# Gate and up projections of a feed-forward layer as seven block products instead of eight

## The chip, the cores and the metric

The kernel runs on one core of one Trainium2 chip. The core has TensorE (PE in the rows, its weight loads PEld), VectorE (DVE), ScalarE (ACT), GpSimd (POOL) and the DMA queue of SyncE (SP). Every engine works through its own list of instructions in order, and the engines meet at semaphores. The metric is the time of one execution on the device in microseconds (us), the median of several runs.

## The reference, cut to what matters

One layer of a hybrid decoder over 528 tokens (16 learned ones in front of 512), width 1024, hidden width 2816:

```python
h = h + mixed @ w_o                       # w_o: 1024 x 1024
gt, up = jnp.split(rms_norm(h, norm2) @ w_gate_up, 2, axis=-1)   # each 512 x 2816
return h + (jax.nn.silu(gt) * up) @ w_down                        # w_down: 2816 x 1024
...
return rms_norm(h, final_norm)[:, N_META:]
```

`mixed` comes from a gated delta rule with eight heads and a short convolution. That part takes some 60% of the time and the change leaves it alone. `rms_norm` multiplies by a factor for each token (the inverse root of the mean square) and by a weight for each channel. The kernel applies the token's factor behind the product: rows of `gt` and `up` are scaled by it, after `h` times the channel weight has gone through TensorE.

## The kernel before, in words

Everything lies transposed: channels on the 128 partitions, tokens along the free axis. A weight block is 1024 inputs by 128 outputs, stored as 128 x 1024: eight tiles (k = 0 to 7) of 128 x 128. The list BLOCKS orders all blocks: projections of the mixers, then eight `wo` blocks (the product with w_o), then 22 pairs of a `gate` and an `up` block. After these MAIN blocks comes the product with w_down, in 22 more blocks of the stream, for eight tiles of output channels (m = 0 to 7) with 22 inner tiles each (k = 0 to 21, one for each pair).

For precision every operand is used as a sum of two fp32r values, a high part and a low part. A product of one weight tile with 512 tokens is then three matmuls of 512 columns (`products`): high weights by high tokens, high by low, low by high. A block is 8 x 3 = 24 matmuls, a pair 48.

A weight block goes through four engines. SP loads it into `w_raw` (three buffers), ACT rounds each half (128 x 512) to `w_hi`, POOL subtracts for `w_lo` (`split_weights` on both, L416 and L330 of the rows), and TensorE waits for the low part of the half. `w_hi` and `w_lo` have two buffers each, so the halves of block n+1 are made while TensorE computes block n.

The loops on ACT, DVE and POOL go through the same n: in each step q = 0 to 3 an engine does a piece of the delta rule, a piece of the evacuation of block n-1 (`evacuate`), and (q = 1, 2) a half of the weights of block n+1. So on ACT the work on the result of block n-1 stands ahead of the weights of block n+1.

The evacuations that matter here: for `wo` block m, DVE adds the result to `h1` (L987), ACT writes the scaled `og_hi` (L626), DVE the low part `og_lo` (L989), ACT the squares `sqt` (L630), which POOL adds up in `sqa`. TensorE sums them over the channels with a matmul of ones (`h_sums`) inside the first `up` block, and ACT makes the token factor `rs2` of it (L418, L419). For `gate`, DVE multiplies by `rs2` (`tg`), ACT takes silu (`sg`, L635), DVE multiplies by `rs2` once more. For `up`, DVE multiplies the result by `sg` (`ff`), ACT rounds to `f_hi` and POOL subtracts for `f_lo` (L380). In the product with w_down, DVE adds each finished tile to `h1` (L1027); the last tile is done in two halves of 256 tokens, so that the final norm of the first half can start early.

## Time and profile before

| | |
|---|---|
| median of 3 runs | 1071.83 us (1071.82 to 1072.09) |
| the profiled execution | 1071.95 us |
| its span (first to last instruction) | 1070.1 us |
| TensorE busy | 1058.5 us, 99% of the span |
| VectorE, ScalarE, GpSimd busy | 417.6, 426.9, 538.3 us |
| TensorE's granted clock over the span | 0.997 of full speed |

The span and what lies around it (1.85 us) make the profiled time. In the rows, a start is counted from the start of the span. The time of a matmul in a row runs from its start to its modelled end, and matmuls overlap; the distance from one start to the next tells what one costs. The same holds, to a smaller degree, for instructions that follow each other on DVE, ACT and POOL.

### The profile page before, as it was taken

Reading aid. Unit: us, or ns where it says so; the run is one execution under the profiler, and the core shown is the slowest. Engines: PE = TensorE matmul, PEld = TensorE weight load, DVE = VectorE, ACT = ScalarE, POOL = GpSimd, SP = SyncE. Lnnn points to the kernel's source line nnn. Section 1 sums busy time; section 2 is a strip of 40 time slices with the busy share of each in tenths; the row PEclk is TensorE's granted clock in tenths of the full one; section 3 lists DMA queues with packets and bytes.
Section 4 is the critical chain, followed back from the end, with each engine's and each line's share of the span. In section 5 each row is a group of like instructions: output and inputs, shape, how many; then the busy total and the mean of one; then the engine's idle time right before and its main releaser. Section 6 shows DMA issues by size and latency. Waiting matters only on the chain.

```text
span 1070.1 us, 20296 instructions
## 1 busy us (share of the span) xinstructions
PE 1058.5 (99%) x8233; PEld 902.9 (84%) x8233; DVE 417.6 (39%) x771; ACT 426.9 (40%) x957; POOL 538.3 (50%) x467
## 2 busy tenths in 40 slices
PE   8999999999999999999999999999999999999996
PEld 8989898989999999978888888878888888888886
DVE  6575757576676767643211122221111211100002
ACT  7736354545545354534222334433223332233222
POOL 0163636363635454453645546755555555555553
PEclk9999999999999999999999999999999999999998
DMA  6221222121222121222522333223222332232222
GB/s 224 71 90 63 70 78 72 60 90 61 76 75 71 61 90 61 73 68 79 177 99 79 99 98 96 84 97 99 99 84 94 99 99 93 86 98 98 99 79 79
DMA packets 28812, 95.44 MB, mean 89 GB/s; under 512 B 2984, under 2 KB 5288, under 8 KB 28720
## 3 DMA queue, kind: packets, MB, share of 16 engines
q1 hardware_dynamic: 27520, 91.77, 26.4%
q10 hardware_dynamic: 1200, 2.38, 0.6%
q8 instruction: 65, 1.06, 0.4%
q14 instruction: 27, 0.22, 0.1%
HBM read 92.03 MB, written 2.11 MB: 88 GB/s over the span
## 4 chain that ended last, share of the span: by engine, by line
PE 97%; ACT 1%; DVE 1%; issue 0%; DMA 0%; DVEq 0%; SPq 0%; ACTq 0%
PE bank L1045 96%; DMA h_in<-h_t 0%; PE bank L1245 0%; PE bank L1239 0%; DVE w_lo L719 0%; ACT w_hi L416 0%; DVE cv L878 0%; DVE raw L708 0%; ACT x_hi L425 0%; ACT L484 0%; ACT L651 0%; DVE h L1036 0%; PE bank L1252 0%; PE bank L1251 0%; ACT qkv L651 0%
## 5 line engine op out<-in xcount | busy, mean ns | idle before, releaser
L330 POOL TENSOR_TENSOR w_lo<-w_raw,w_hi 128x512 fp32r<-128x512 f32 x312 | 410.2, 1332 | 480.7 <-ACT w_hi L416 480.6
L1045 PE MATMUL bank<-x_hi,w_hi 128*128 128x258 f32 (+2 forms) x896 | 247.7, 334 | 0.4 <-DVE w_lo L719 0.4
L1045 PE MATMUL bank<-x_hi,w_lo 128*128 128x258 f32 (+2 forms) x896 | 230.1, 315 | 0.0
L1045 PE MATMUL bank<-x_lo,w_hi 128*128 128x258 f32 (+2 forms) x896 | 228.0, 315 | 0.0
L416 ACT ACTIVATE w_hi<-w_raw 128x512 fp32r<-128x512 f32 x322 | 187.6, 618 | 91.8 <-PE bank L1045 91.6
L1045 PE MATMUL bank<-og_hi,w_hi 128*128 128x512 f32 x416 | 164.7, 396 | 0.0
L1045 PE MATMUL bank<-og_lo,w_hi 128*128 128x512 f32 x416 | 164.3, 395 | 0.0
L1045 PE MATMUL bank<-og_hi,w_lo 128*128 128x512 f32 x416 | 164.3, 395 | 0.0
L1045 PEld LDWEIGHTS bank<-x_hi,w_lo 128*128 128x128 f32 x896 | 147.3, 189 | 11.3
L1045 PEld LDWEIGHTS bank<-x_hi,w_hi 128*128 128x128 f32 x896 | 146.0, 189 | 12.4 <-DVE w_lo L719 0.7
L1045 PEld LDWEIGHTS bank<-x_lo,w_hi 128*128 128x128 f32 x896 | 146.3, 189 | 8.9
L1045 PEld LDWEIGHTS bank<-og_lo,w_hi 128*128 128x128 f32 x416 | 78.0, 187 | 19.3 <-issue 0.2
L1045 PEld LDWEIGHTS bank<-og_hi,w_hi 128*128 128x128 f32 x416 | 78.0, 187 | 19.2 <-issue 0.2
L1045 PEld LDWEIGHTS bank<-og_hi,w_lo 128*128 128x128 f32 x416 | 78.0, 187 | 19.2
L878 DVE SCALAR_TENSOR_TENSOR cv<-raw,sm,cv 128x528 f32<-128x528 f32 (+1 forms) x72 | 70.4, 978 | 3.5 <-ACT cv L607 2.1
L1045 PE MATMUL bank<-f_hi,w_hi 128*128 128x512 f32 (+1 forms) x182 | 68.8, 378 | 0.0
L1045 PE MATMUL bank<-f_lo,w_hi 128*128 128x512 f32 (+1 forms) x182 | 68.7, 377 | 0.0
L1045 PE MATMUL bank<-f_hi,w_lo 128*128 128x512 f32 (+1 forms) x182 | 68.6, 377 | 0.0
L708 DVE TENSOR_TENSOR tg<-bank,rs 128x512 f32<-128x512 f32 x22 | 15.2, 690 | 110.2 <-PE bank L1045 101.7
L1045 PE MATMUL bank<-yb_hi,w_hi 128*128 128x512 f32 x128 | 51.5, 403 | 0.0
L1045 PE MATMUL bank<-yb_lo,w_hi 128*128 128x512 f32 x128 | 50.5, 395 | 0.0
L1045 PE MATMUL bank<-yb_hi,w_lo 128*128 128x512 f32 x128 | 50.5, 395 | 0.0
(263 smaller groups left out, 1295.7 us busy)
## 6 DMA issues: line engine op xcount, KB each, us to landing
w_raw<-w_stream SPq DMA_DIRECT2D x162, 512.0 KB, 3.3
h_in<-h_t SPq DMA_DIRECT2D x4, 528.0 KB, 7.2
h<-h_t ACTq DMA_DIRECT2D x1, 2048.0 KB, 11.2
h_in<-gc_dram SPq DMA_DIRECT2D x7, 264.0 KB, 3.2
out<-h SPq DMA_DIRECT2D x4, 256.0 KB, 3.1
out<-h SPq DMA_DIRECT2D x2, 384.0 KB, 2.6
cst<-consts SPq DMA_DIRECT2D x1, 512.0 KB, 8.5
h_in<-gc_dram ACTq DMA_DIRECT2D x1, 264.0 KB, 3.0
```

The lines of the kernel that those rows point to most:

```text
L330: nc.gpsimd.tensor_tensor(low_weights(n)[:, at], w_raw[:, n % 3, at], high_weights(n)[:, at].bitcast(f32), ALU.subtract).then_inc(wlo_read ...
L416: return nc.scalar.activation(to, x, ACT.Copy)
L708: return nc.vector.tensor_tensor(to, a, b, ALU.mult)
L878: ins = nc.vector.scalar_tensor_tensor(to, xj, taps[:, j:j + 1], to, ALU.mult, ALU.add)
L1045: return nc.tensor.matmul(o, w, x, start=start, stop=stop)
```

## The change

For each pair m the gate block and the up block are stacked to a weight matrix of 256 outputs by 1024 inputs, cut in four quarters: gate (1) or up (2) by first half of the inputs (k = 0 to 3) or second half (k = 4 to 7). They are called "11", "12", "21", "22", and each is 128 x 512. The tokens' matrix is cut in four as well: input half by token half of 256. The eight block products of the plain form become seven (`PRODUCTS`), for which four sums of weight quarters ("s1" to "s4") and four sums of token quarters ("t1" to "t4") are made. A block product is 4 tiles x 3 = 12 matmuls of 256 columns, a pair 84. Seven additions (`join`) make gate and up from the seven results.

- Sums of the tokens' quarters are made once, while the `wo` blocks are evacuated: `xp` is the scaled `h1`; its differences, high parts and low parts take the place of L626 and L989.
- Sums of the weights are made by DVE for each pair (`weight_sum`). The high part of each of the seven weight parts is made by ACT (`part_high`), the low part by POOL for products 1, 3 and 6 of a pair and by DVE for 0, 2, 4 and 5 (`part_low`). There are four buffers of a part; the high part p may be written when product p-4 is done.
- A product writes the first half of one of the eight banks; a bank comes round again after eight products, and TensorE waits for the addition that read it (`joined`). ACT copies the first product's result (`copy_first`).
- `w_raw` has a fourth buffer, in the constants' place (`cst`).
- The second multiplication by `rs2` is left out of the gate and done on the result of the w_down product instead (`sg`, then a subtraction from `h1`, since the sign of f is turned).
- f is kept in full precision (`f_full`), and is split in high (ACT, `f_split`) and low parts (DVE, `f_low`) only from the last pair on: k = 0 to 5 inside it, k = 6 to 21 behind it.

```diff
+PRODUCTS = ("11", "s1", "s2", "12", "s3", "s4", "22")
+NP = len(PRODUCTS)
+EARLY_F = 12
+ON_POOL = [0] + [NP * m + i for m in range(FT) for i in (1, 3, 6)]
+ON_DVE = [p for p in range(NP * FT) if p not in ON_POOL]
...
+        def weight_source(p):
+            m, i = divmod(p, NP)
+            return (quadrants(m) | {"s1": pair_sums[:, 0, :], "s2": pair_sums[:, 1, :], "s3": quadrants(m)["21"],
+                                    "s4": pair_sums[:, 0, :]})[PRODUCTS[i]]
+        def part_of(p, flat_weights):
+            return flat_weights[:, 512 * (p % 4):512 * (p % 4) + 512]
+        def product_out(p):
+            return bank[(p + 6) % 8][:, 0:QUARTER]
...
+            def part_low(p):
+                pool.wait_ge(ph_ready, p + 1)
+                nc.gpsimd.tensor_tensor(part_of(p, w_lo_flat), weight_source(p), part_of(p, w_hi_flat).bitcast(f32),
+                                        ALU.subtract).then_inc(pl_pool, 1)
...
+            for p in ON_POOL:
+                part_low(p)
+                if p == 3:
+                    evacuate(FFN - 1, *BLOCKS[FFN - 1])
...
+            def part_high(p):
+                m, i = divmod(p, NP)
+                name = PRODUCTS[i]
+                if p >= 4:
+                    act.wait_ge(prod_done, p - 3)
+                elif p == 2:
+                    act.wait_ge(half_block, 1)
+                else:
+                    act.wait_ge(block_done, FFN if p == 3 else FFN - 1)
+                if name[0] == "s":
+                    act.wait_ge(sum_made, sums_made(m, name))
+                else:
+                    wait_raw_loaded(act, FFN + 2 * m + int(name[0]) - 1)
+                copy(part_of(p, w_hi_flat), weight_source(p)).then_inc(ph_ready, 1)
+            def copy_first(m):
+                act.wait_ge(prod_done, NP * m + 1)
+                if m:
+                    act.wait_ge(joined, join_number(m - 1, "c11"))
+                copy(p1_part, product_out(NP * m)).then_inc(part_copied, 1)
...
+            def f_split(k):
+                act.wait_ge(f_ready, k + 1)
+                if k >= EARLY_F:
+                    act.wait_ge(prod_done, NP * (FT - 1) + 3)
+                copy(f_high(k), f_full[:, k, :]).then_inc(fhi_ready, 1)
...
+            for m in range(FT):
+                p = NP * m
+                part_high(p + 3)
+                if m == 0:
+                    scaled_x(KT - 1)
+                else:
+                    silu_gate(m - 1)
+                copy_first(m)
+                if m == 0:
+                    x_high(KT - 1, "t2")
+                    x_high(KT - 1, "2x")
+                part_high(p + 4)
+                if m == 0:
+                    x_high(KT - 1, "t3")
+                    x_high(KT - 1, "t4")
+                    square_h1(KT - 1)
+                part_high(p + 5)
+                part_high(p + 6)
+                for i in range(3):
+                    if m < FT - 1:
+                        part_high(p + 7 + i)
+                    else:
+                        f_split(2 * i)
+                        f_split(2 * i + 1)
+                        split_weights(MAIN + i // 2, i % 2)
+                if m == 0:
+                    act.wait_ge(h_sums, 1)
+                    inverse_root(rs2[:, :], dbank[1][:, :], 1.0 / D, 0).then_inc(rs2_ready, 1)
+            split_weights(MAIN + 1, 1)
+            silu_gate(FT - 1)
+            for k in range(6, FT):
+                f_split(k)
...
+                    add_h1(m)
+                    dve.wait_ge(xp_ready, m + 1)
+                    if m < 4:
+                        half_difference(m)
+                        x_low(m, "11")
+                        x_low(m, "t1")
                     else:
+                        for name in ("t2", "t3", "t4"):
+                            x_sum(m, name)
+                        for name in ("t2", "2x", "t3", "t4"):
+                            x_low(m, name)
...
+            def weight_sum(m, name):
+                w = quadrants(m)
+                if name == "s1":
+                    wait_raw_loaded(dve, FFN + 2 * m + 1)
                     if m:
+                        wait_part_low(dve, NP * (m - 1) + PRODUCTS.index("s4"))
+                    to, a, b = pair_sums[:, 0, :], w["21"], w["22"]
+                if name == "s2":
+                    wait_raw_loaded(dve, FFN + 2 * m)
+                    dve.wait_ge(sum_made, sums_made(m, "s1"))
+                    if m:
+                        wait_part_low(dve, NP * (m - 1) + PRODUCTS.index("s2"))
+                    to, a, b = pair_sums[:, 1, :], pair_sums[:, 0, :], w["11"]
+                if name == "s3":
+                    dve.wait_ge(sum_made, sums_made(m, "s1"))
+                    to, a, b = w["21"], w["21"], w["11"]
+                if name == "s4":
+                    dve.wait_ge(sum_made, sums_made(m, "s2"))
+                    wait_part_low(dve, NP * m + PRODUCTS.index("s1"))
+                    to, a, b = pair_sums[:, 0, :], pair_sums[:, 1, :], w["12"]
+                nc.vector.tensor_tensor(to, a, b, ALU.add).then_inc(sum_made, 1)
+            def part_low(p):
+                dve.wait_ge(ph_ready, p + 1)
+                nc.vector.tensor_tensor(part_of(p, w_lo_flat), weight_source(p), part_of(p, w_hi_flat).bitcast(f32),
+                                        ALU.subtract).then_inc(pl_dve, 1)
+            def join(m, name):
+                product, part, to, uses = {
+                    "v": (2, p1_part, v_part, None), "w": (1, v_part, w_part, "v"), "c11": (3, p1_part, tg[:, 0:QUARTER], None),
+                    "u": (4, v_part, c2[:, 0:QUARTER], "v"), "c22": (4, w_part, c2[:, QUARTER:T], "w"),
+                    "c12": (5, w_part, tg[:, QUARTER:T], "w"), "c21": (6, c2[:, 0:QUARTER], c2[:, 0:QUARTER], "u")}[name]
+                dve.wait_ge(prod_done, NP * m + max(product, 2 if name == "w" else 0) + 1)
+                if name == "v":
+                    dve.wait_ge(part_copied, m + 1)
+                if uses:
+                    dve.wait_ge(joined, join_number(m, uses))
+                nc.vector.tensor_tensor(to, product_out(NP * m + product), part, ALU.add).then_inc(joined, 1)
...
+            def f_low(k):
+                dve.wait_ge(fhi_ready, k + 1)
+                nc.vector.tensor_tensor(f_lo[:, k, :], f_full[:, k, :], f_high(k).bitcast(f32), ALU.subtract).then_inc(flo_ready, 1)
+            for m in range(FT):
+                p = NP * m
+                if m:
+                    weight_sum(m, "s3")
+                    join(m - 1, "c21")
+                weight_sum(m, "s4")
+                if m:
+                    gate_up(m - 1)
+                    part_low(p + 4)
+                part_low(p + 5)
+                join(m, "v")
+                join(m, "w")
+                if m < FT - 1:
+                    weight_sum(m + 1, "s1")
+                if m:
+                    dve.wait_ge(sg_ready, m)
+                join(m, "c11")
+                if m < FT - 1:
+                    part_low(p + 7)
+                else:
+                    f_low(0)
+                    f_low(1)
+                if m:
+                    dve.wait_ge(f_ready, m)
+                join(m, "u")
+                join(m, "c22")
+                if m < FT - 1:
+                    weight_sum(m + 1, "s2")
+                else:
+                    f_low(2)
+                    f_low(3)
+                join(m, "c12")
+                if m < FT - 1:
+                    part_low(p + 9)
+                scaled_gate(m)
+            join(FT - 1, "c21")
+            f_low(4)
+            f_low(5)
+            gate_up(FT - 1)
+            for k in range(6, FT):
+                f_low(k)
...
+                    link(mult(sg[:, :], big[m % 2][0][:, :], rs2[:, :]))
+                    nc.vector.tensor_tensor(h1[:, m, :], h1[:, m, :], sg[:, :], ALU.subtract).then_inc(h2_ready, 1)
...
+            def part_product(p, name, x_waits):
+                wait_part_low(pe, p)
+                high, low = part_of(p, w_hi_flat), part_of(p, w_lo_flat)
+                x_h, x_l = x_operand[name]
+                for k in range(4):
+                    if k in x_waits:
+                        pe.wait_ge(xlow_made, x_waits[k])
+                    at = slice(128 * k, 128 * (k + 1))
+                    mm(product_out(p), high[:, at], x_h[:, k, :], start=k == 0, stop=False)
+                    mm(product_out(p), high[:, at], x_l[:, k, :], start=False, stop=False)
+                    ins = mm(product_out(p), low[:, at], x_h[:, k, :], start=False, stop=k == 3)
+                ins.then_inc(prod_done, 1)
+            for m in range(FT):
...
+                for i, name in enumerate(("11", "t1", "t2", "21", "t3", "22", "t4")):
+                    if p + i in (2, 4):
+                        pe.wait_ge(h1_ready, KT - 1 if i == 2 else KT)
+                    elif p + i == 6:
+                        pe.wait_ge(sqa_ready, KT)
+                        mm(dbank[1][:, :], ones, sqa[:, :]).then_inc(h_sums, 1)
+                    elif p + i == 7:
+                        pe.wait_ge(rs2_ready, 1)
+                    elif m and i == 1:
+                        pe.wait_ge(part_copied, m)
+                    elif m and i:
+                        pe.wait_ge(joined, join_number(m - 1, ("w", "v", "c11", "c22", "c12")[i - 2]))
+                    elif m >= 2:
+                        pe.wait_ge(joined, join_number(m - 2, "c21"))
+                    part_product(p + i, name, x_waits.get(i, {}))
```

What the change does to the list of VectorE, first before, at the begin of the gate and up stage (from here on it repeats with each pair; `tg`, `sg` and `ff` are the gate, its silu and the result of the pair):

```order
L989 SCALAR_TENSOR_TENSOR og_lo<-h,sm,og_hi 128x512 [waits hnhi_ready]
L708 TENSOR_TENSOR tg<-bank,rs 128x512 [waits rs2_ready,block_done]
L708 TENSOR_TENSOR sg<-sg,rs 128x512 [waits sg_ready]
L708 TENSOR_TENSOR ff<-bank,sg 128x512 [waits sg2_ready,block_done]
L708 TENSOR_TENSOR tg<-bank,rs 128x512 [waits sg_ready,block_done]
L708 TENSOR_TENSOR sg<-sg,rs 128x512 [waits sg_ready]
L708 TENSOR_TENSOR ff<-bank,sg 128x512 [waits sg2_ready,flo_ready,block_done]
```

In the same stage after, most of one pair, from the weights' fourth sum on; L1213 is `weight_sum`, L1216 `part_low`, L1228 `join`, L876 the two multiplications:

```order
L1213 TENSOR_TENSOR pair_sums<-pair_sums,w_raw 128x512 [waits pl_pool,sum_made]
L876 TENSOR_TENSOR f_full<-c,sg 128x512 [waits joined,sg_ready]
L1216 TENSOR_TENSOR w_lo<-w_raw,w_hi 128x512 [waits ph_ready]
L1216 TENSOR_TENSOR w_lo<-pair_sums,w_hi 128x512 [waits ph_ready]
L1228 TENSOR_TENSOR parts_mem<-bank,parts_mem 128x256 [waits part_copied,prod_done]
L1228 TENSOR_TENSOR parts_mem<-bank,parts_mem 128x256 [waits joined,prod_done]
L1213 TENSOR_TENSOR pair_sums<-cst 128x512 [waits pl_dve,w_in3]
L1228 TENSOR_TENSOR tg<-bank,parts_mem 128x256 [waits prod_done,sg_ready]
L1216 TENSOR_TENSOR w_lo<-w_raw,w_hi 128x512 [waits ph_ready]
...
L1213 TENSOR_TENSOR pair_sums<-pair_sums,w_raw 128x512 [waits pl_dve,sum_made,w_in2]
L1228 TENSOR_TENSOR tg<-bank,parts_mem 128x256 [waits joined,prod_done]
L1216 TENSOR_TENSOR w_lo<-pair_sums,w_hi 128x512 [waits ph_ready]
```

Three instructions for each pair have become seventeen, and TensorE and ACT wait for most of them.

ScalarE's list around the end of the first `wo` block, before (L416 of `w_hi` is `split_weights`):

```order
L416 ACTIVATE yb_hi<-cbuf 128x512 [waits yb_ready,block_done]
L416 ACTIVATE w_hi<-w_raw 128x512 [waits block_done,w_in2] x2
L671 ACT_TABLE_LOAD
L626 ACTIVATE og_hi<-h,sm 128x512 [waits h1_ready,block_done]
L630 ACTIVATE sqt<-h 128x512
L416 ACTIVATE w_hi<-w_raw 128x512 [waits block_done,w_in0] x2
```

and after, for m = 4 to 6, where `xp` is L560 and the four further instructions are high parts of the tokens' quarters:

```order
L560 ACTIVATE xp<-h,sm 128x512 [waits h1_ready,block_done]
L511 ACTIVATE xe<-tq 128x256 [waits t_made]
L566 ACTIVATE og_hi<-h,sm 128x2x256
L511 ACTIVATE og_hi<-tq 128x256 [waits t_made] x2
L575 ACTIVATE sqt<-h 128x512 [waits sqa_ready]
L511 ACTIVATE w_hi<-w_raw 128x512 [waits block_done,w_in2] x2
```

The high parts of the next block's weights have moved behind four more instructions, three of which wait for VectorE.

## Rows read from the trace of the kernel before

**Rows 1.** The page: busy time by engine, and the chain that ended last.

```profile
PE 1058.5 (99%) x8233; PEld 902.9 (84%) x8233; DVE 417.6 (39%) x771; ACT 426.9 (40%) x957; POOL 538.3 (50%) x467
...
PE 97%; ACT 1%; DVE 1%; issue 0%; DMA 0%; DVEq 0%; SPq 0%; ACTq 0%
```

**Rows 2.** Busy time by stretch: wo, gate and up, w_down, the end.

```profile
core 0: us, PE busy (x) PEld busy (x) DVE busy (x) ACT busy (x) POOL busy (x), PEclk, DMA share, GB/s
644.07:688.86 44.79, 44.79 (x194) 35.98 (x192) 12.18 (x17) 18.98 (x32) 28.49 (x24) 1.00 0.30 94
688.86:936.13 247.27, 247.27 (x1060) 198.32 (x1059) 46.38 (x67) 77.03 (x136) 140.24 (x111) 1.00 0.29 94
...
1060.90:1070.10 9.20, 0.71 (x3) 0.30 (x2) 2.37 (x4) 1.61 (x4) 1.27 (x1) 0.67 0.37 126
```

**Rows 3.** Timeline of TensorE (start, us, operation) at the stage's ends and h_sums.

```profile
688.86 0.40 PE L1045 MATMUL bank<-og_hi,w_hi 128*128 128x512 f32 x1
...
697.26 1.02 PE L1045 MATMUL bank<-sqa,ones_mem 128*128 128x512 f32 x2
...
698.36 0.40 PE L1045 MATMUL bank<-og_lo,w_hi 128*128 128x512 f32 x1
...
936.13 0.40 PE L1045 MATMUL bank<-f_hi,w_hi 128*128 128x512 f32 x1
```

**Rows 4.** Timeline of TensorE, 256 columns: first and 34th of an unbroken stretch.

```profile
1044.97 0.28 PE L1045 MATMUL bank<-f_hi,w_hi 128*128 128x256 f32 x1
...
1048.82 0.28 PE L1045 MATMUL bank<-f_hi,og_hi 128*128 128x256 f32 x1
```

**Rows 5.** Groups by shape: count | busy us, mean ns of one | idle before.

```profile
L416 ACT ACTIVATE h_in<-bank 128x256 f32<-128x256 f32 x32 | 11.9, 372 | 12.1 <-PE bank L1045 12.1
```

**Rows 6.** Timelines of DVE: four of 512 columns unblocked, two of 264 from a bank.

```profile
7.54 2.50 DVE L719 TENSOR_TENSOR w_lo<-w_raw,w_hi 128x512 fp32r<-128x512 f32 x4 [7.54 <-ACT w_hi L416]
...
35.26 0.77 DVE L708 TENSOR_TENSOR raw<-bank,rs_mem 128x264 f32<-128x264 f32 x2
...
454.37 0.42 DVE L830 TENSOR_TENSOR um<-um,bank 128x256 f32<-128x256 f32 x1
454.82 0.71 DVE L833 STREAM_TRANSPOSE tm<-um 128x512 f32<-128x512 f32 x1
```

**Rows 7.** Timelines of DVE and of POOL in the same microseconds.

```profile
442.09 0.68 DVE L708 TENSOR_TENSOR xt<-xt,cst 128x512 f32<-128x512 f32 x1
442.70 0.68 DVE L708 TENSOR_TENSOR kd_vb<-bank,h_in 128x512 f32<-128x512 f32 x1
443.30 1.18 DVE L868 TENSOR_TENSOR osq<-osq,h_in 128x512 f32<-128x512 f32 x1
...
442.31 1.61 POOL L330 TENSOR_TENSOR w_lo<-w_raw,w_hi 128x512 fp32r<-128x512 f32 x1 [0.69 <-ACT w_hi L416]
```

**Rows 8.** All engines but TensorE behind the end of the first wo block.

```profile
649.87 0.69 DVE L987 TENSOR_TENSOR h<-bank,h 128x512 f32<-128x512 f32 x1 [1.66 <-PE bank L1045]
650.65 0.72 ACT L626 ACTIVATE og_hi<-h,sm 128x512 fp32r<-128x512 f32 x1 [0.83 <-DVE h L987]
651.28 0.61 ACT L630 ACTIVATE sqt<-h 128x512 f32<-128x512 f32 x1
651.41 0.75 DVE L989 SCALAR_TENSOR_TENSOR og_lo<-h,sm,og_hi 128x512 fp32r<-128x512 f32 x1 [0.85 <-ACT og_hi L626]
651.80 1.14 ACT L416 ACTIVATE w_hi<-w_raw 128x512 fp32r<-128x512 f32 x2
652.50 2.54 POOL L330 TENSOR_TENSOR w_lo<-w_raw,w_hi 128x512 fp32r<-128x512 f32 x2 [1.88 <-ACT w_hi L416]
```

**Rows 9.** Timeline of ACT: the token factor rs2 and the first silu.

```profile
698.38 0.69 ACT L418 ACTIVATE rs<-bank,eps 128x512 f32<-128x512 f32 x1 [2.51 <-PE bank L1045]
699.10 0.63 ACT L419 ACTIVATE rs<-rs 128x512 f32<-128x512 f32 x1
```

**Rows 10.** Timeline of DVE and ACT behind the last matmuls.

```profile
1060.95 0.42 DVE L1031 TENSOR_TENSOR h<-bank,h 128x256 f32<-128x256 f32 x1 [2.80 <-PE bank L1045]
1061.41 0.42 ACT L695 ACTIVATE sqt<-h 128x256 f32<-128x256 f32 x1 [4.89 <-DVE h L1031]
```

329 lines of the change are left out of this document (229 added, 100 removed).

## The prediction, made from these rows

> **What bounds the kernel now.** I read the busy times and the chain first: TensorE is busy for 1058.5 of 1070.1 us and carries 97% of the chain that ended last [rows 1]. Then the busy times by stretch: gate and up take 247.27 us, from 688.86 to 936.13, with TensorE never idle at a granted clock of 1.00, while DVE is busy for 46.4 us of them and POOL for 140.2 [rows 2]. The timeline gives the inside of this stage: the sums matmul and its refill take 698.36 - 697.26 - 0.23 = 0.87 us, so 22 x 48 matmuls of 512 columns took 246.4 us, 0.2333 us each, 11.20 us a pair [rows 3]. What TensorE saves counts in full, as long as the others deliver.
>
> **TensorE's share.** In an unbroken stretch with 256 columns, 33 matmuls start in 3.85 us, 0.1167 us each, half of 0.2333 [rows 4]. A pair becomes 84 x 0.1167 = 9.80 us, a product 1.40. With nothing else in the way the stage would lose 22 x 1.40 = 30.8 us.
>
> On this place the Trainium skill bears ("TensorE: Matmul & The Clock Gate", section "LDWEIGHTS (loading the stationary operand)"): it gives a weight load as columns / 1.2 ns, 107 ns for 128, and the change needs 84 loads for 48. If these could not hide behind 256 columns, a pair would take 84 x (107 + 107) ns, an estimate by that page of 18 us, and the change would be lost. The even 0.1167 us, each with its own load, speaks against it.
>
> **VectorE's share, which decides.** Each pair now gives DVE seventeen instructions: ten of 512 columns with both inputs in SBUF (four sums, four low parts, the two multiplications), and seven additions of 256 columns with one input from a bank. Four of the first kind took 2.50 us, the last ending 0.69 after its start: 0.605 from start to start [rows 6]. Two of 264 columns from a bank took 0.77, so one takes 0.345 [rows 6]. One that needs the one before it starts 0.45 behind it, as L833 behind L830 [rows 6]. That makes 10 x 0.605 + 7 x 0.345 + 0.105 ("w" needs "v") = 8.57 us, within 9.80.
>
> Two waits come on top. The first is POOL. At 442.31 POOL began a subtraction while DVE ran one of the first kind; DVE's ended at 442.77 and POOL's at 443.92, 1.15 later, in 1.61 instead of 1.27 us. DVE's next, with one input from a bank (442.70), took its normal 0.68. The one after it, with both inputs in SBUF, began at 443.30 and ended at 444.48, 0.56 behind POOL's end [rows 7]. So the two exclude each other, and only the additions from banks run beside POOL. A POOL subtraction between two DVE ones of the first kind spreads their ends from 0.605 to 1.15 + 0.56 = 1.71 us: it costs 1.105, less what additions lie between. POOL has three for each pair. I place them by the chain ACT high part (0.62 and 0.03 to 0.09 of hand-over, as 651.80 to 652.50 shows [rows 8]) to POOL:
>
> - Product 6's begins behind the second low part. "v" and "w" (0.795) follow; then the sum s1 is late by 1.71 - 1.40 = 0.31.
> - Product 1's of the next pair needs s1, so its chain ends during the low part of product 0. "u" and "c22" (0.69) follow; s2 is late by 1.71 - 1.295 = 0.415.
> - Product 3's comes 0.535 behind the high part of product 2 and meets that part's subtraction and the multiplication of `tg` by `rs2`, with no addition between: 1.105.
>
> The second wait is DVE's own: product 2's low part needs s2, which lies only one addition ahead. From the place where the next instruction could follow s2, it is 0.085 to its end (0.69 - 0.605), 0.08 of hand-over to ACT (650.56 to 650.65), the copy's 0.62 and 0.03 back (651.37 to 651.41) [rows 8], 0.815 together, of which "c12" covers 0.345: 0.47. ACT itself has some 5 us of work for a pair, seven copies at 0.535, a silu and one copy of 256 columns from a bank, at most 0.37 [rows 5]; it is no bound. The sum is 8.57 + 1.83 + 0.47 = **10.87 us a pair**. DVE is the new bound, and TensorE waits some 1.1 us for the fifth product's low part. Break-even of the stage alone is 11.20.
>
> The cost of a POOL meeting has the bounds 0 (it always falls beside additions) and 1.105, so a pair lies between 9.80 and 12.36; I take the order worked out above, as each request comes 0.06 or more inside the neighbour.
>
> **The stage from end to end.** The first product's low part is late (below), 0.9 us. In the first pair ACT and DVE also do the tokens' quarters of the last `wo` block; the sum s4 and product 5 come 1.5 us late. Product 7 has the bank of the channel sums and waits for `rs2`. ACT makes that behind the high part of product 9, which needs s2, at the end of DVE's list: about 14.7 us, plus 0.69 and 0.63 with 0.03 between for the two steps [rows 9], brings product 7 to 16.4 us after the stage's begin. DVE is then free of arrears. The second pair runs at 9.8, the third at 10.3, in the fourth the fifth product begins 6.75 after the pair's begin, 18 periods later (195.7) it is that of the last pair, and its three products take 4.2. Sum: 243.15 against 247.27, **-4.1 us**.
>
> **The `wo` blocks.** After a block's end (644.07 + 24 x 0.2333 = 649.67 [rows 2, 3]) the low part of the next block's first half is ready at 653.77, 1.5 before it is needed at 655.27 [rows 8]. For m = 4 to 6 ACT gets one wait for DVE (about 0.5) and four copies for one (1.5 net) ahead of the weights. That is 2.0 against 1.5, with meetings of DVE and POOL on top: 0.8 late, of which the first two times fall here and the third is the 0.9 above. **+1.7 us** (0 to 3).
>
> **The begin of w_down.** Before, POOL subtracted for f pair by pair. Now DVE does k = 4 to 21 behind the last pair, with a last join and two multiplications: 18 x 0.605 + 1.55 = 12.4 us, begun some 2.2 us behind TensorE's begin (the last additions), with about four meetings of 1.1 for the weights of the first three blocks: the last is ready at about 18.9. TensorE wants it after 21 x 0.70 = 14.7. **+4.2 us** (0 to 6).
>
> **The end.** A multiplication and its hand-over are added to the last half, 0.42 + 0.03 [rows 10]: **+0.45 us**. For the first half the same lies beside matmuls. The six tiles before it have a whole tile's time.
>
> **Sum.** 1071.95 (the profiled execution, span 1070.1 and 1.85 around it) - 4.1 + 1.7 + 4.2 + 0.45 = 1074.2. The median of the runs is 0.12 lower: **1074.0 us**. A change within 0.2% (1069.7 to 1074.0) can't be told from none by a measurement of this kernel.
>
> **Rivals.**
>
> - *DVE keeps the port.* No row shows two independent DVE instructions of the first kind in a row with POOL waiting: in rows 7 an addition from a bank stood between. A DVE instruction starts 0.085 before the last ends [rows 6]; if that is enough to go first, product 3's subtraction waits for the addition "c21", which covers 0.345. A pair takes 10.52, the stage 6.3 us less: 1067.7. Chance 0.25. The Trainium skill ("SBUF — State Buffer", section "Who interferes with whom") has it that issue order decides who blocks; POOL would have issued first here, and the forecast would stand. Rows 7 agree where POOL was first (443.30).
> - *TensorE stays the bound.* This needs meetings and the s2 wait to shrink below 1.23 us together: 247.3 - 30.8 + 3 for `rs2` = 219.5, 27.8 less, and the other terms +4: about 1048. Against it: rows 7. Chance 0.07.
> - *Slower: hand-overs on DVE.* All seventeen instructions wait for semaphores, eleven for two or three. I took satisfied waits as free, since 443.30 had two and still came 0.60 behind 442.70 [rows 7]. If each costs 0.03, as a hand-over does, a pair takes 11.4 and 18 periods cost 9.2 more: 1083. With the other terms as above it turns the result slower from 10.75 a pair on. Chance 0.27.
> - *The clock.* TensorE would stand for 1.1 us in each pair, and the only low clock in the rows, 0.67, is the last stretch, where it works 0.71 of 9.2 us [rows 2]. At half clock a pair takes 19.6; I give it 0.02: over 1150.
> - *The change isn't what it says*: if the seven products were not 84 matmuls of 256 columns, TensorE's rows would show it; DVE's bound would be the same. Chance 0.01.
>
> **How the numbers follow.** The forecast has 0.38. It spreads by 0.4 us a pair and by the transitions' bounds, so it lies on both sides: 0.09 below 1069.7, 0.12 within, 0.17 above. *DVE keeps the port* adds 0.22 faster and 0.03 within, TensorE's bound 0.07 faster, the hand-overs 0.27 slower, the last two 0.03 slower. Together: faster 0.38, same 0.15, slower 0.47. The range 1061 to 1087 takes in the first and third rival and leaves out TensorE's bound, the clock, and a pair over 11.6.
>
> **What the profile after would show.** The spacing of 256 columns, 0.117: the matmuls' term. TensorE's idle time in the stage, named after DVE's low parts: the bound. DVE's busy share there near 0.9 and single L1213 and L1216 of 1.2 us instead of 0.69: the meetings. A distance of 10.9 between pairs: the sum. A wait of about 3 us before the second pair: `rs2`. `flo` waits of 4 us behind the stage. The forecast is wrong if DVE waits for TensorE in the steady part, or if a pair is under 10.5 or over 11.3.

## The result, and the profile after

The changed kernel takes 1079.82 us (median of 4 runs, 1079.1 to 1080.79) against 1071.82 (4 runs): a ratio of 1.0075, 95% interval 1.0057 to 1.0092. The profiled execution took 1080.42 us with a span of 1078.6, 8.5 more than before.

From the page: busy time by engine, and the chain that ended last.

```profile
PE 1039.0 (96%) x9025; PEld 925.3 (86%) x9025; DVE 638.4 (59%) x1141; ACT 482.8 (45%) x1069; POOL 499.2 (46%) x424
...
PE 76%; DVE 16%; issue 4%; ACT 3%; DMA 0%; POOL 0%; DVEq 0%; ACTq 0%; SPq 0%; POOLq 0%
```

TensorE has 20 us less to do than in [rows 1], and its share of the chain fell from 97% to 76%. VectorE has 16% of it now.

Busy time by stretch, as in [rows 2]: the `wo` blocks, gate and up, the first tile of w_down, and two pieces of that tile.

```profile
644.07:690.77 46.70, 45.08 (x192) 35.52 (x191) 24.43 (x44) 27.47 (x52) 27.90 (x23) 1.00 0.32 102
690.77:936.69 245.92, 224.68 (x1851) 219.76 (x1851) 231.27 (x379) 116.12 (x213) 98.36 (x70) 0.99 0.29 95
936.69:960.24 23.55, 18.10 (x69) 13.18 (x68) 16.48 (x25) 13.33 (x24) 11.20 (x7) 0.93 0.26 84
951.30:954.39 3.09, 0.20 (x1) 0.00 (x1) 1.90 (x4) 2.61 (x4) 3.09 (x2) 1.00 0.00 0
954.39:958.30 3.91, 3.91 (x10) 3.12 (x11) 0.00 (x0) 0.00 (x0) 3.65 (x3) 0.56 0.38 130
```

The `wo` blocks end 1.9 us later than before. Gate and up take 245.92 us instead of 247.27, so the whole stage saved 1.35 us; VectorE is busy for 94% of it. The first tile of w_down takes 23.55 us, where 66 matmuls of 0.2333 take 15.4 before [rows 3]: 8.15 more. With -0.3 at the end, where the last half's added multiplication is outweighed by a shorter last transfer, these make the 8.5 us within 0.1.

Timeline of TensorE: starts that had a wait ahead of them, up to the second pair, and one of the steady part. Two more, 0.82 us at 685.09 and 0.76 at 697.35, are left out.

```profile
678.44 0.47 PE L1344 MATMUL bank<-yb_hi,w_hi 128*128 128x512 f32 x1 [0.79 <-DVE h L1167]
...
692.14 0.51 PE L1344 MATMUL bank<-xe,w_hi 128*128 128x256 f32 x2 [1.21 <-POOL w_lo L417]
...
702.36 0.39 PE L1344 MATMUL bank<-og_hi,w_hi 128*128 128x256 f32 x1 [1.57 <-DVE w_lo L1216]
708.66 0.60 PE L1344 MATMUL bank<-xe,w_hi 128*128 128x256 f32 x2 [2.35 <-ACT rs L514]
...
802.17 0.36 PE L1344 MATMUL bank<-og_hi,w_hi 128*128 128x256 f32 x1 [0.81 <-DVE w_lo L1216]
```

The last row comes back in every pair from the third on: the fifth product waits for VectorE's low part, from the fourth pair on 0.73 to 0.82 us. With the 1.57 of the first pair and 0.17 of the third these are 16.9 us in 21 waits. Behind the 2.35 us wait at 708.66 the granted clock was 0.55 for 3.76 us: 18 matmuls of 256 columns, 0.21 us apart, 1.66 us more than at 0.1167. In the steady pairs it was 1.00.

Timelines of VectorE, and of GpSimd, in one steady pair.

```profile
796.88 0.69 DVE L1216 TENSOR_TENSOR w_lo<-pair_sums,w_hi 128x512 fp32r<-128x512 f32 x1 [0.42 <-ACT w_hi L511]
797.49 1.79 DVE L876 TENSOR_TENSOR tg<-tg,rs 128x512 f32<-128x512 f32 x1
799.21 0.68 DVE L1213 TENSOR_TENSOR cst<-cst,w_raw 128x512 f32<-128x512 f32 x1
...
803.40 0.92 DVE L1213 TENSOR_TENSOR pair_sums<-w_raw 128x512 f32<-128x512 f32 x1
...
805.84 1.12 DVE L1213 TENSOR_TENSOR pair_sums<-pair_sums,w_raw 128x512 f32<-128x512 f32 x1
...
808.34 1.79 DVE L876 TENSOR_TENSOR tg<-tg,rs 128x512 f32<-128x512 f32 x1
```

```profile
797.45 1.28 POOL L417 TENSOR_TENSOR w_lo<-w_raw,w_hi 128x512 fp32r<-128x512 f32 x1 [1.88 <-ACT w_hi L511]
```

From one multiplication of `tg` to the next, 797.49 to 808.34, lie 10.85 us: the period. VectorE stands still for 0.42 us only, ahead of the low part of product 2. Three instructions that would take 0.68 take 1.79, 0.92 and 1.12: they meet GpSimd's three subtractions.

The begin of w_down: VectorE's last low parts of f; GpSimd; TensorE; ScalarE.

```profile
947.11 6.10 DVE L1272 TENSOR_TENSOR f_lo<-f_full,xe 128x512 fp32r<-128x512 f32 x10
```

```profile
951.03 4.54 POOL L413 TENSOR_TENSOR w_lo<-w_raw,w_hi 128x512 fp32r<-128x512 f32 x2 [10.15 <-ACT w_hi L511]
```

```profile
954.39 0.57 PE L1344 MATMUL bank<-xe,w_hi 128*128 128x512 f32 x1 [2.89 <-POOL w_lo L413]
```

```profile
945.12 5.31 ACT L511 ACTIVATE xe<-f_full 128x512 fp32r<-128x512 f32 x10
950.34 1.14 ACT L511 ACTIVATE w_hi<-w_raw 128x512 fp32r<-128x512 f32 x2
```

ScalarE puts the high parts of the third w_down block behind all splits of f. GpSimd is ready at 951.03; two subtractions take it 4.54 us instead of the 2.54 of [rows 8]. VectorE meanwhile goes through ten of its own at 0.605 without a gap, to 953.21. TensorE waits 2.89 us, and behind that wait its granted clock is 0.56 for 3.9 us, where the nine matmuls from 954.39 to 958.14 take 3.75 us instead of 2.10: 1.65 us more.

### The profile page after: what moved, and what is told of

Read it like the earlier page. It is cut to its first block, busy times and chain, and to the rows that moved or that the text cites. A ratio compares the mean times of both kernels' runs of the same rounds, so it can differ in the third digit from the quotient of the medians.

```text
span 1078.6 us, 22661 instructions
## 1 busy us (share of the span) xinstructions
PE 1039.0 (96%) x9025; PEld 925.3 (86%) x9025; DVE 638.4 (59%) x1141; ACT 482.8 (45%) x1069; POOL 499.2 (46%) x424
## 4 chain that ended last, share of the span: by engine, by line
PE 76%; DVE 16%; issue 4%; ACT 3%; DMA 0%; POOL 0%; DVEq 0%; ACTq 0%; SPq 0%; POOLq 0%
PE bank L1344 75%; DVE pair_sums L1213 3%; DVE tg L876 3%; DVE w_lo L1216 2%; DVE c L1228 2%; ACT w_hi L511 2%; DVE f_full L876 1%; DVE w_raw L1213 1%; DVE cst L1213 1%; DVE f_lo L1272 0%; DMA h_in<-h_t 0%; PE bank L1544 0%; PE bank L1538 0%; POOL w_lo L413 0%; DVE og_lo L1192 0%
## 5 line engine op out<-in xcount | busy, mean ns | idle before, releaser
L413 POOL TENSOR_TENSOR w_lo<-w_raw,w_hi 128x512 fp32r<-128x512 f32 x214 | 290.6, 1373 | 369.9 <-ACT w_hi L511 369.8
L511 ACT ACTIVATE w_hi<-w_raw 128x512 fp32r<-128x512 f32 x290 | 171.7, 618 | 71.9 <-PE bank L1344 71.5
L1344 PE MATMUL bank<-og_hi,w_hi 128*128 128x256 f32 (+1 forms) x416 | 125.8, 302 | 16.9 <-DVE w_lo L1216 16.9
L1344 PE MATMUL bank<-xe,w_hi 128*128 128x256 f32 (+1 forms) x602 | 125.1, 297 | 7.2 <-POOL w_lo L413 2.9
L1344 PE MATMUL bank<-og_hi,w_lo 128*128 128x256 f32 (+1 forms) x416 | 123.8, 298 | 0.0
L1344 PE MATMUL bank<-og_lo,w_hi 128*128 128x256 f32 (+1 forms) x416 | 123.6, 297 | 0.0
L1344 PEld LDWEIGHTS bank<-xe,w_hi 128*128 128x128 f32 x602 | 96.2, 191 | 12.0 <-POOL w_lo L413 3.3
L1344 PE MATMUL bank<-xe,w_lo 128*128 128x256 f32 (+1 forms) x338 | 104.0, 308 | 0.0
L417 POOL TENSOR_TENSOR w_lo<-w_raw,w_hi 128x512 fp32r<-128x512 f32 x34 | 47.7, 1403 | 75.3 <-ACT w_hi L511 75.3
L511 ACT ACTIVATE w_hi<-pair_sums 128x512 fp32r<-128x512 f32 x66 | 41.8, 633 | 86.9 <-DVE pair_sums L1213 83.4
L1344 PEld LDWEIGHTS bank<-xe,w_lo 128*128 128x128 f32 x338 | 64.9, 192 | 3.3
```

What stands on the lines that cost most here:

```text
L413: nc.gpsimd.tensor_tensor(low_weights(n)[:, at], raw_weights(n)[:, at], high_weights(n)[:, at].bitcast(f32), ALU.subtract).then_inc(wlo_re ...
L417: nc.gpsimd.tensor_tensor(part_of(p, w_lo_flat), weight_source(p), part_of(p, w_hi_flat).bitcast(f32), ALU.subtract).then_inc(pl_pool, 1)
L511: return nc.scalar.activation(to, x, ACT.Copy)
L1344: return nc.tensor.matmul(o, w, x, start=start, stop=stop)
```

## The experiments

My theory was the prediction's: VectorE's list sets the period, and of it some 1.8 us are meetings with GpSimd. The rival was that the time between pairs comes from the number of hand-overs, or from TensorE itself.

**Take the meetings away.** From the second pair on, GpSimd's subtractions are 16 columns wide, so most of three of the seven low parts is left out.

```diff
-                nc.gpsimd.tensor_tensor(part_of(p, w_lo_flat), weight_source(p), part_of(p, w_hi_flat).bitcast(f32),
-                                        ALU.subtract).then_inc(pl_pool, 1)
+                width = slice(0, 512 if p < NP else 16)
+                nc.gpsimd.tensor_tensor(part_of(p, w_lo_flat)[:, width], weight_source(p)[:, width],
+                                        part_of(p, w_hi_flat)[:, width].bitcast(f32), ALU.subtract).then_inc(pl_pool, 1)
```

> From the second pair on, GpSimd's three subtractions of a pair are 16 columns wide instead of 512 (the rest of these low parts is left out, so the products of these parts lack a term); everything waits as before. In the changed kernel a pair takes 10.85 us, and in one pair three VectorE instructions with both inputs in SBUF last 1.79, 1.12 and 0.92 us instead of 0.69. Theory (the two engines exclude each other, VectorE is the bound through these meetings): the meetings shrink to about 0.1, VectorE needs 8.57 + 0.42 us, TensorE becomes the bound, a pair takes 9.80 us, the stage is about 21 x 1.05 = 22 us shorter, the time about 1057. Rival (VectorE is slowed by its seventeen hand-overs or by something else than GpSimd): the pair stays above 10.5 and the time above 1072.

Measured: 1057.17 us, one execution. Timeline of VectorE, `tg`:

```profile
738.05 0.68 DVE L877 TENSOR_TENSOR tg<-tg,rs 128x512 f32<-128x512 f32 x1
747.85 0.68 DVE L877 TENSOR_TENSOR tg<-tg,rs 128x512 f32<-128x512 f32 x1
```

The period is 9.80 us, TensorE's 84 x 0.1167. So the meetings are what lifts the pair above TensorE, and matmuls and hand-overs are not.

**Who goes first.** A copy of one column on ScalarE ahead of product 3's high part delays GpSimd's request into the multiplication of `tg`. It writes to `tick`, a new tensor of one column declared behind `eps`.

```diff
+                if m:
+                    copy(tick[:, :], eps[:, 0:1])
                 part_high(p + 3)
```

> One copy of a single column is added on ScalarE ahead of the high part of product 3, so GpSimd's subtraction for product 3 is asked for some 0.1 to 0.2 us later. In the changed kernel it starts at 797.45, 0.04 us ahead of the multiplication of tg (797.49), which then takes 1.79 us; behind the last pair, on the other hand, ten VectorE instructions in a row kept a waiting GpSimd out for 2.2 us. Theory A (a queued VectorE instruction goes ahead of a waiting GpSimd; GpSimd only won because it asked in the gap): GpSimd now waits until the addition c21, the meeting costs 0.74 instead of 1.11, a pair takes 10.5 us and the time is about 7 us below the changed kernel's, 1073, although work was added. Theory B (whoever waits comes next, as the prediction had it): the pair stays at 10.85 and the time at 1080.

Measured: 1077.8 us (1076.9 to 1078.62), ratio 1.0053 (1.0036 to 1.007). VectorE, and GpSimd:

```profile
796.71 0.68 DVE L879 TENSOR_TENSOR tg<-tg,rs 128x512 f32<-128x512 f32 x1
797.32 1.78 DVE L1216 TENSOR_TENSOR cst<-cst,w_raw 128x512 f32<-128x512 f32 x1
```

```profile
796.76 1.79 POOL L418 TENSOR_TENSOR w_lo<-w_raw,w_hi 128x512 fp32r<-128x512 f32 x1 [1.96 <-ACT w_hi L512]
```

GpSimd asks 0.05 behind the start of `tg`, waits for its end, and goes next, though the sum "s3" stood ready on VectorE. The period stays (10.87): the same 1.1 us, paid one instruction later. The 2 us that this kernel is faster were not expected. Between the profiled executions it is 2.4: 1.8 in w_down, whose tiles took 15.11 us instead of 15.40 (more at e7_pad), and 0.6 before it. There the first product starts 0.64 us later, but the second pair lasts 11.26 us from `tg` to `tg` instead of 12.79, since TensorE's clock stayed at 1.00 behind the same wait of 2.35 us.

**More room between s2 and its low part.** "s3" is moved from the next pair's begin to right behind "s2".

```diff
-                    weight_sum(m, "s3")
                     join(m - 1, "c21")
...
                     weight_sum(m + 1, "s2")
+                    weight_sum(m + 1, "s3")
```

> The weights' sum s3 of the next pair is moved ahead, from behind the multiplication of tg to right behind s2, where VectorE waits 0.42 us in each pair for ScalarE's copy of s2. With theory A (queued VectorE instructions go first) the wait goes, and GpSimd's request for product 3 falls inside the low part of product 2, so that it waits for the addition c21: 10.85 - 0.42 - 1.11 + 0.74 = 10.05 us a pair, about 16 us less in all, 1064. With theory B only the wait goes: 10.43 a pair, about 8 us less, 1072. If the wait isn't on the path (TensorE or ScalarE set the pace): 1080.

Measured: 1070.64 us (1069.28 to 1072.27, 10 runs), ratio 0.9987 (0.9977 to 0.9996). VectorE, and GpSimd:

```profile
793.95 1.78 DVE L876 TENSOR_TENSOR tg<-tg,rs 128x512 f32<-128x512 f32 x1
...
804.34 1.78 DVE L876 TENSOR_TENSOR tg<-tg,rs 128x512 f32<-128x512 f32 x1
```

```profile
804.21 1.36 POOL L417 TENSOR_TENSOR w_lo<-w_raw,w_hi 128x512 fp32r<-128x512 f32 x1 [1.88 <-ACT w_hi L511]
```

The period is 10.38 us, 0.47 less: the wait for ScalarE is gone at its predicted price, and the meeting is not. One moved line brings the changed kernel level with the one before.

**The third w_down block earlier.** ScalarE makes its high parts amid the splits of f, and VectorE waits for GpSimd at two places of its row of ten.

```diff
             for k in range(6, FT):
                 f_split(k)
+                if k == 13:
+                    split_weights(MAIN + 2, 0)
+                    split_weights(MAIN + 2, 1)
...
             for k in range(6, FT):
+                if k in (14, 19):
+                    wait_low(dve, MAIN + 2, int(k == 19))
                 f_low(k)
```

> Behind the last pair, ScalarE makes the high parts of the third block of w_down after f's part 13 instead of after part 21, and VectorE waits for GpSimd's low parts of this block before its own parts 14 and 19 of f, which opens a gap for GpSimd. In the changed kernel TensorE waits 2.9 us there for GpSimd (951.5 to 954.4) and then runs nine matmuls at half clock (1.75 us more). Theory (the wait comes from GpSimd being kept out by VectorE's unbroken row, and the low clock from the wait): the two, 4.65 us, shrink to about 1.1, the time is about 3.5 us below the changed kernel's. Rival (the delay only moves to VectorE's own parts of f, since both have the same work to do): under 1.5 us gained.

Measured: 1078.69 us, one execution. VectorE, and GpSimd:

```profile
947.08 1.28 DVE L1275 TENSOR_TENSOR f_lo<-f_full,xe 128x512 fp32r<-128x512 f32 x2
949.56 8.14 DVE L1275 TENSOR_TENSOR f_lo<-f_full,xe 128x512 fp32r<-128x512 f32 x8 [1.20 <-POOL w_lo L413]
```

```profile
946.84 3.92 POOL L413 TENSOR_TENSOR w_lo<-w_raw,w_hi 128x512 fp32r<-128x512 f32 x2 [5.98 <-ACT w_hi L511]
```

The wait of 2.89 us and the low clock are gone, but VectorE's last subtraction ends at 957.7 instead of 953.2, and TensorE now waits for it three times (1.29, 0.34 and 0.65). From the first matmul of w_down to its first finished tile on VectorE go 22.1 us instead of 23.75. That is what the rival in the expectation had said: ScalarE's order alone is a small part of the 8 us. The larger one, as far as this run tells, is that two engines' subtractions have to go one after the other.

**The stage's begin.** ScalarE's weights ahead of its evacuations in the `wo` blocks (and product 0's high part before the last block's end), and `rs2` ahead of product 9's high part.

```diff
-                    weights_first = BLOCKS[n][0] in ("c", "u")
+                    weights_first = BLOCKS[n][0] in ("c", "u") or AT["wo", 1] <= n < FFN
...
+                    if m == 0 and i == 2:
+                        act.wait_ge(h_sums, 1)
+                        inverse_root(rs2[:, :], dbank[1][:, :], 1.0 / D, 0).then_inc(rs2_ready, 1)
                     if m < FT - 1:
                         part_high(p + 7 + i)
```

> Both waits around the stage's begin that come from ScalarE's order are taken away: the high parts of the wo blocks stand ahead of each block's closing chores (and the first product's high part before the last block ends), and the second normalisation's inverse root stands before the third of the next pair's high parts. If the order is the cause, TensorE's waits of 0.79 and 0.82 us at the wo blocks and most of the 1.21 us before the first product go (-2 to -2.8), and of the 2.35 us before the second pair about 1.5 goes: 1079.8 - 4 = 1075.5, 1074.5 to 1077. If VectorE's low parts are late whatever the order is (rival), the first waits stay and less than 1.5 us in all comes back: 1078.3 or more. The pair stays at 10.85 us either way.

Measured: 1077.51 us (1076.63 to 1077.84), ratio 1.0054 (1.0037 to 1.0071). TensorE, the start of the first product:

```profile
692.78 0.50 PE L1345 MATMUL bank<-xe,w_hi 128*128 128x256 f32 x2 [3.39 <-POOL w_lo L417]
```

This is 2.3 us less than the changed kernel, where 4 were expected. The waits at 678 and 685 are gone, and the first product starts 0.64 us later than before all the same: GpSimd has a sum of squares ahead of that low part. The order at `wo` gave nothing. The second pair's `tg` comes 2.6 us earlier (718.91 for 721.50). Of this 0.7 is `rs2` itself (the first `tg` at 708.05 for 708.71). The other 1.9 is the pair behind it, 10.86 us instead of 12.79: TensorE has no wait ahead of it now, and its clock stays at 1.00.

**The place in memory.** One column that nothing reads or writes, declared behind `eps`. The built program puts tensors at multiples of 32 bytes, so all later ones move by 32 bytes, the tokens' operands among them; `w_hi` and `w_lo` stay.

```diff
         eps = sb("eps", [128, 2])
+        sb("pad", [128, 1])
```

> Nothing is changed but one tensor of one column (four bytes a partition), never read or written, that stands behind eps and moves every later tensor in memory. In e2_tick, which had such a tensor, the tiles of w_down took 15.11 us instead of 15.40, matmuls 0.2289 us apart instead of 0.2333, and nobody had meant that. Theory A, the place of the operands in memory sets the spacing: here too 15.1 us a tile, 7.4 tiles, so about 2 us less than 1079.8: 1077.7. Theory B, it was the added copy on ScalarE or chance of that build: 15.40 us a tile and 1079.8.

Measured: 1078.81 us (1077.23 to 1078.98), ratio 1.0062 (1.0047 to 1.0077). Timeline of VectorE, the evacuations of two w_down tiles, 15.11 us apart, and the same of the changed kernel without the column, 15.39 apart:

```profile
990.93 0.69 DVE L877 TENSOR_TENSOR sg<-bank,rs 128x512 f32<-128x512 f32 x1 [13.69 <-PE bank L1345]
1006.04 0.69 DVE L877 TENSOR_TENSOR sg<-bank,rs 128x512 f32<-128x512 f32 x1 [12.62 <-PE bank L1345]
```

```profile
991.24 0.69 DVE L876 TENSOR_TENSOR sg<-bank,rs 128x512 f32<-128x512 f32 x1 [13.98 <-PE bank L1344]
1006.63 0.69 DVE L876 TENSOR_TENSOR sg<-bank,rs 128x512 f32<-128x512 f32 x1 [12.95 <-PE bank L1344]
```

The place sets the spacing: 0.2289 us instead of 0.2333. That settles the 1.8 us of e2_tick in w_down; this kernel's second pair had the low clock again (12.78 us), and its median is 1.0 us below the changed kernel's, e2_tick's 2.0.

**One subtraction less on GpSimd.** The kernel with "s3" moved, and product 3's low part on VectorE, behind `tg`.

```diff
-ON_POOL = [0] + [NP * m + i for m in range(FT) for i in (1, 3, 6)]
+ON_POOL = [0] + [NP * m + i for m in range(FT) for i in (1, 3, 6) if m == 0 or i != 3]
...
+                    part_low(p + 3)
                     join(m - 1, "c21")
```

> e3_s3 with the low part of product 3 (the one whose subtraction on GpSimd meets the multiplication tg on VectorE) moved from GpSimd to VectorE, straight behind that multiplication, from the second pair on. Theory A, a meeting costs VectorE as much as GpSimd's whole hold of the port: the pair loses 1.1 us of meeting and gains one subtraction of 0.605, 10.38 - 0.5 = 9.88 us, just above TensorE's 9.80: 21 pairs give 10.5 us less than e3_s3's 1070.6: 1060.2, and TensorE's waits nearly vanish. Theory B, the cost of meetings is not bound to that one request: the two requests that are left fall on other instructions of VectorE and cost more than they do now (0.25 and 0.45 us), so that the pair is 10.4 us or longer and the time 1070.5 or more.

Measured: 1060.15 us (1058.19 to 1061.52), ratio 0.989 (0.9875 to 0.9905). Timeline of VectorE:

```profile
790.11 0.68 DVE L876 TENSOR_TENSOR tg<-tg,rs 128x512 f32<-128x512 f32 x1
790.71 0.68 DVE L1216 TENSOR_TENSOR w_lo<-w_raw,w_hi 128x512 fp32r<-128x512 f32 x1
...
799.95 0.68 DVE L876 TENSOR_TENSOR tg<-tg,rs 128x512 f32<-128x512 f32 x1
```

The period is 9.84 (e3_s3: 10.38), and TensorE waits nowhere in the steady part. VectorE got more to do and the pair became shorter: 0.605 of work for 1.1 of meeting.

**What keeps GpSimd out.** First, an addition of one column before each of the last six subtractions of the row; then two satisfied waits there instead.

```diff
             for k in range(6, FT):
+                if k >= 16:
+                    nc.vector.tensor_tensor(sm[:, ALOG + k - 16:ALOG + k - 15], eps[:, 0:1], eps[:, 1:2], ALU.add)
                 f_low(k)
```

> An addition of one column on VectorE stands before each of the last six of the ten subtractions f_lo that run without a gap, and kept GpSimd's first subtraction for the third block of w_down waiting (from 951.03 to about 953.2). Theory A, only an unbroken row of instructions of one kind keeps GpSimd out, as the two cases in the pairs say where it came in between two different instructions: GpSimd comes in at about 951.5, its result is there near 952.7, TensorE waits 1.2 us instead of 2.9 and keeps its full clock: 3 us less, 1076.8. Theory B, any work of VectorE that is ready keeps it out: wait and half clock stay, 1079.8 to 1080.3.

Measured: 1078.51 us, one execution. VectorE, and GpSimd:

```profile
951.54 0.67 DVE L1272 TENSOR_TENSOR f_lo<-f_full,xe 128x512 fp32r<-128x512 f32 x1
952.15 1.22 DVE L1314 TENSOR_TENSOR sm<-eps 128x1 f32<-128x1 f32 x1
953.29 0.68 DVE L1272 TENSOR_TENSOR f_lo<-f_full,xe 128x512 fp32r<-128x512 f32 x1
```

```profile
951.64 3.49 POOL L413 TENSOR_TENSOR w_lo<-w_raw,w_hi 128x512 fp32r<-128x512 f32 x2 [10.14 <-ACT w_hi L511]
```

GpSimd comes in at the first boundary, ahead of a small addition that takes 1.22 us for it. TensorE waits 1.31 us instead of 2.89, the clock stays at 1.00, and w_down's first tile is ready 21.3 us after its begin instead of 23.75.

```diff
+                if k >= 16:
+                    dve.wait_ge(tg_ready, FT)
+                    dve.wait_ge(sg_ready, FT)
                 f_low(k)
```

> The changed kernel with two more waits, both long satisfied, on each of the last six f_lo subtractions of the unbroken row on VectorE, and no addition between them. In e9_row additions of one column at the same places let GpSimd in at the next of them. Theory A, any place where VectorE's list has more to look at than the next subtraction opens the port: GpSimd's first low part for the third w_down block (asked at about 951.0) runs at once behind the subtraction in progress and is ready near 952.6, TensorE waits 1.3 us there instead of 2.9, no half clock follows, 1077.3 to 1078.5. Theory B, satisfied waits are free and leave the row unbroken, as in the pairs of the steady part where instructions with two and three waits follow each other 0.60 us apart: the subtraction is ready at 954.3, the wait is 2.9 us, the clock falls to half behind it, 1079.8.

Measured: 1080.24 us (1079.93 to 1080.56), ratio 1.0079 (1.0049 to 1.0108). VectorE, and GpSimd:

```profile
947.32 6.10 DVE L1272 TENSOR_TENSOR f_lo<-f_full,xe 128x512 fp32r<-128x512 f32 x10
```

```profile
951.26 4.54 POOL L413 TENSOR_TENSOR w_lo<-w_raw,w_hi 128x512 fp32r<-128x512 f32 x2 [10.16 <-ACT w_hi L511]
```

Satisfied waits cost nothing and open nothing: ten subtractions with up to three waits each still take 6.10 us.

**All together, and the kernel before.** e10_best is e8_less with the early `rs2`, the small additions and the column of e7_pad. e11_more is e8_less with the other edits: ScalarE's order at `wo` with GpSimd's first low part ahead of its sum of squares, the early `rs2`, e4_down's edit, and 16 columns (64 bytes). e12_before_pad is the kernel before with one column.

> e8_less with three edits of the other runs added: the inverse root before the third of the next pair's high parts (of e5_wo_rs2), the additions of one column in the row of f_lo (of e9_row), and the tensor of one column that moves the later ones (of e7_pad). If their gains add up: -3 at the second pair, -1 at w_down's begin (in e8_less TensorE waited there for GpSimd 0.47 us only, and had its half clock at another place), -2 by matmuls 0.2289 us apart in w_down: 1060.15 - 6 = 1054, 1053 to 1056. If the second pair is held by something else once the root is early, as product 0 was in e5_wo_rs2, -1 at most from it: 1056 to 1057.5.

> e8_less with the other version of each: ScalarE's order at the wo blocks with, now, GpSimd's first low part ahead of its last sum of squares (in e5_wo_rs2 that low part was what TensorE waited 3.39 us for), the early root, the high parts of the third w_down block amid the f splits (of e4_down), and an unused tensor of 16 columns, 64 bytes, instead of one. If GpSimd's order was what held product 0: TensorE's waits at 678 and 685 are gone and product 0 waits less than 1.5 us: 1060.15 - 3 - 2 - 1 = 1054 without any gain by the memory place, 1052 with it. If VectorE's work is what is behind (rival), product 0 still waits 2.5 us or more: 1056. On the place: with 64 bytes either 15.4 us a tile in w_down (only a shift that is no multiple of 64 bytes matters) or 15.1 (any shift).

> The kernel before with the unused tensor of one column alone. If the place in memory sets the spacing of the 512-column matmuls of w_down in any kernel: 15.1 instead of 15.4 us a tile, 1069.8, and perhaps less where the gate and up blocks gain too (44 blocks of 5.6 us, up to 4.6 us more). If the effect belongs to the layout of the changed kernel alone: 15.4 us a tile and 1071.9.

Measured: e10_best 1053.12 us (1052.85 to 1053.3), ratio 0.9822 (0.9807 to 0.9836); e11_more 1060.67 (1060.18 to 1061.46), 0.9895 (0.9878 to 0.9911); e12_before_pad 1064.64 (1064.4 to 1065.01), 0.993 (0.9915 to 0.9945). e10_best came as expected, with 9.84 us for the second pair instead of 12.82 in e8_less. e11_more missed by 5 us and more. With GpSimd's low part first, the first product starts at 689.10 without a wait, but the second one waits 2.31 us for GpSimd's next low part, and behind that wait its matmuls are 0.21 us apart until 696.5. The larger loss is in the pairs, which take 10.08 us instead of 9.84 with TensorE never idle: its matmuls stand further apart with all later tensors 64 bytes on. A group of TensorE's matmuls in e10_best between 720 and 905 us (count | busy us, mean ns | idle before), and e12_before_pad's evacuations of two w_down tiles:

```profile
L1348 PE MATMUL bank<-og_hi,w_hi 128*128 128x256 f32 x304 | 85.1, 280 | 0.0
```

```profile
991.32 0.69 DVE L1028 TENSOR_TENSOR h<-bank,h 128x512 f32<-128x512 f32 x1 [14.41 <-PE bank L1046]
1006.43 0.69 DVE L1028 TENSOR_TENSOR h<-bank,h 128x512 f32<-128x512 f32 x1 [14.42 <-PE bank L1046]
```

TensorE has no idle time in these pairs; it is the bound in e10_best, at 9.89 us a pair, against 9.84 in e8_less. The column took 7.5 us off the kernel before: 0.2289 holds for its gate and up blocks too, which is 22 x 48 x 0.0044 = 4.6 us, beside 2.1 in w_down and 0.7 in the `wo` blocks, which end at 688.12 instead of 688.86 (5.49 us a block instead of 5.60). In the changed kernel it could give little but w_down's share, since VectorE was the bound in the pairs. So the place in memory is worth nearly as much as the change costs, and it has to be the same on both sides of a comparison: with the column on both, the change is 1.3% slower (1078.81 to 1064.64), and e10_best 1.1% faster.

## Why the prediction came out as it did

**Matmuls.** 0.1167 us for 256 columns held: twelve matmuls of a product are 1.40 us apart from the next in e1_thin, where nothing else limits. The doubt about 84 weight loads is gone.

**The pair.** 10.87 us predicted, 10.85 measured, and the parts agree: meetings 0.245, 0.445 and 1.115 (0.31, 0.415 and 1.105), and 0.42 of visible wait behind "s2" with 0.05 of hand-over (0.47; its removal gave 0.47). e3_s3 and e8_less took single terms away, and each moved the period by its price (0.47 for 0.47, 0.54 for 1.115 less the 0.605 added); e1_thin took away all meetings and came to TensorE's bound.

**The rivals.** *DVE keeps the port* fell in the pairs: in e2_tick GpSimd asked second and still went ahead of a ready addition. But the row in which VectorE does keep it exists, one stage later, where I had not looked for it. *Hand-overs on DVE* fell: eleven of the instructions wait for more than one semaphore and still follow each other at 0.60, and e13_waits adds twelve waits at no cost. *TensorE stays the bound* is what the kernel becomes once one subtraction is moved. The clock stayed at full speed in the steady pairs with their 0.81 us waits.

**The stage's end to end.** -4.1 predicted, -1.35 measured. The step that failed: "the second pair runs at 9.8". The second pair begins 17.9 us after the stage, not 16.4 (of this the first product is 0.5: 1.37 late, not 0.9), and then takes 11.54 us on TensorE. Timeline of VectorE, the second pair, in the changed kernel and in e2_tick:

```profile
708.71 0.69 DVE L876 TENSOR_TENSOR tg<-tg,rs 128x512 f32<-128x512 f32 x1 [0.61 <-ACT rs L514]
...
713.99 0.69 DVE L1216 TENSOR_TENSOR w_lo<-pair_sums,w_hi 128x512 fp32r<-128x512 f32 x1 [0.78 <-ACT w_hi L511]
...
721.50 1.79 DVE L876 TENSOR_TENSOR tg<-tg,rs 128x512 f32<-128x512 f32 x1
```

```profile
709.35 0.69 DVE L879 TENSOR_TENSOR tg<-tg,rs 128x512 f32<-128x512 f32 x1 [0.61 <-ACT rs L515]
...
720.61 0.69 DVE L879 TENSOR_TENSOR tg<-tg,rs 128x512 f32<-128x512 f32 x1
```

Behind its wait for `rs2` TensorE ran at half clock and was 1.66 us late after 18 matmuls. ScalarE may write the high part of the pair's sixth product only when the second is done, so VectorE waits 0.78 for it, and GpSimd's next request meets the sum s1 later and in full (1.68 us instead of 0.92). From `tg` to `tg` that makes 12.79 us, and the next pairs run at 10.87 at once. In e2_tick the wait for `rs2` is the same on both engines, the clock stays at 1.00, and the pair lasts 11.26: the low clock cost 1.5 us. The wait of VectorE's own multiplication for `rs2` is only 0.61. The prediction had a wait of about 3 us before the second pair among its signs, and a low clock among its rivals, but put no price on the one behind the other. The third pair took 10.29 us on TensorE, as reckoned (10.3).

**The `wo` blocks.** +1.7 predicted, +1.9 measured, by the mechanism named: two waits of 0.8 behind ScalarE's longer list. The profile puts them down to VectorE's addition to `h` (678.44, L1167), but that one is for the block just ended, and a block waits only for the result of the one before that. What it does wait for is GpSimd's low part, begun at 677.02 and done near 678.3; in e10_best the same two waits are put down to it (1.10 and 0.92 us), and in e5_wo_rs2, with ScalarE's weights first, they are gone. That undoing it moves the loss to the first product instead was not foreseen.

**The begin of w_down**, the term that was mis-sized: +4.2 predicted, +8.15 measured. VectorE's list was even shorter than reckoned (its last low part of f is there 16.5 us after the begin, not 18.9). What I missed is that this list is not what ends last. TensorE waits 0.73 and 1.75 us for f's low parts at the start, where GpSimd's four subtractions lie between VectorE's; 2.89 for GpSimd, which ScalarE's order starts late and VectorE's unbroken row keeps out; and pays 1.65 for the half clock behind that. These are 7.0; the rest is in gaps below 0.5 us, most of them beside these waits. No run took the first two waits away. I had priced one engine's list with its meetings, and not followed the other two lists to the same point.

**The end.** +0.45 predicted; the multiplication did cost 0.46 (1069.72 to 1070.18), and the last transfer landed about 0.7 earlier.

The total came out 6 us above the forecast, within its range and with the sign held likeliest: -4.1 was 2.8 too good and +4.2 was 4 too small. About 3.2 of these 6 us (1.5 and 1.65) are half clock behind a long wait of TensorE, which the sum had at nothing. That the time lies in the range says little, since the range was 26 us wide; what the runs bear out is the pair.
